# A second MLP's norm: an activation table loaded earlier, a residual summed one quarter at a time, and idle transposes in between

## The chip, the cores and the metric

The kernel runs on one core of one Trainium2 chip. The metric is the device time in microseconds (us) of one execution. The kernel before takes 2209.97 us, the median of three runs (2206.25 to 2210.57 us).

## What is computed

Two transformer layers one after the other, on 256 tokens of width 2048, in float32. The first is a hybrid mixer with an MLP; the second is this one, and the change sits at the seam between its attention and its MLP:

```python
def rmsnorm_2(x, g):
    xf = x.astype(jnp.float32)
    y = xf * lax.rsqrt(jnp.mean(xf * xf, axis=-1, keepdims=True) + EPS)
    return (y * g.astype(jnp.float32)).astype(x.dtype)

def sqrelu_mlp(x, w1, w2):
    return (jnp.square(jax.nn.relu(x @ w1)) @ w2).astype(x.dtype)

def second_block(x, ...):
    h = rmsnorm_2(x, norm_g[i, 0])
    h = fox_attention(h, fox_w_in[j], fox_b_f[j], fox_w_out[j])
    x = x + rmsnorm_2(h, norm_g[i, 1])
    h = sqrelu_mlp(rmsnorm_2(x, norm_g[i, 2]), mlp_w1[i], mlp_w2[i])
    x = x + rmsnorm_2(h, norm_g[i, 3])
```

So between the attention's last product (`fox_w_out`) and the MLP's first product (`mlp_w1`) there stand a norm of h over all 2048 columns, a sum, and the turning of x so that its columns lie on the partitions. The MLP's own norm (`norm_g[i, 2]`) is applied as a gain while x is turned; its root is put in later, on the MLP's output.

## The kernel before, in words

**Products.** A float32 product is made of three passes over parts in a reduced type: each weight is split into a high part (`wh`, ScalarE, `hi`, L634) and a low part (`wl`, VectorE, `lo`, L1155), and so are the activations (`XH` and `XL`, kept together as `XHL`). Weights come in chunks of 128x2048 (1 MB). There are four chunk slots, j = 0 to 3, and four chunks make one panel of 512 output columns. `raw` and `wl` share their memory, so a slot's next chunk is fetched by SyncE only when the product has used the slot (`chunk_used`). A panel's result stands in a pair of PSUM banks, `acc[o % 2]`.

**Order.** Every engine's order is written out by hand; the engines meet at semaphores, and each engine works strictly down its own list. `B_FOUT` are the four panels of `fox_w_out`; `B_M2` is the first panel of `mlp_w1`.

**The seam, engine by engine.** After the last `fox_w_out` matmul:
- ScalarE squares the last 512 columns straight from PSUM (`squares(2, 3)`, L677 and L678), takes the square root (`root`, L641), and then, for each quarter of x, copies the turned blocks with their gain into `XH` (`take_quarter`, L655). In between it makes the high parts of chunks 1, 2 and 3 (`hi`, L637). Chunk 0 is ready already.
- VectorE adds the squares up (L1173, L1174), multiplies the last panel of h by its gain (`fox_panel(3)`, L1928), takes the reciprocal (L1183), adds h to x in quarters of 512 columns (`fox_added`, L1937), and makes the low parts of the turned blocks (`low_quarter`, L1192) and of the chunks (L1158).
- TensorE turns x. A quarter is two pairs of blocks, eight transposes (`turn_quarter`, L2112). Then it runs the panel: sixteen k-tiles, each of twelve matmuls (L2066 to L2068), four k-tiles to a chunk.

In `first_panel` of before, for this MLP (m = 3, so `late` is false), quarters 0 and 1 are turned before the product, quarter 2 after chunk 0 and quarter 3 after chunk 1. Ahead of each chunk the product waits for both pairs of its quarter and for the chunk's low part:

```python
                for j in range(4):
                    wait_emptied(pe, ("xt", m, 2 * j))
                    wait_emptied(pe, ("xt", m, 2 * j + 1))
                    form(b, j, o % 2, j == 0, j == 3, 4 * j)
                    if not late and j < 2:
                        turn_quarter(m, j + 2)
```

ScalarE's order there is: take quarter 0, `hi` of chunk 1, take quarters 1 and 2, `hi` of chunk 2, take quarter 3, `hi` of chunk 3. VectorE's `lo` of chunk 2 stands behind its low parts of quarter 2, and `lo` of chunk 3 behind those of quarter 3. The change leaves these stretches as they are.

Of the kernel before, what the change touches and what calls it, by code (L numbers as in the profile page):

```python
# [18 lines left out]
P = 128  # L19
TOK = 256  # L20
NT = TOK // P
D = 2048
KT = D // P
# [41 lines left out]
ACT = mybir.ActivationFunctionType  # L65
# [5 lines left out]
def hybrid_then_fox(nc, x, g_mix, w_in, conv_w, conv_b, dt_bias, a_log, d_skip, g_ssd, g_q, g_k,  # L71
# [3 lines left out]
    with ctx:  # L75
        def sem(name):
            return ctx.enter_context(nc.semaphore(name))

        def sb(name, shape, dt=F32):
            return ctx.enter_context(nc.sbuf_tensor(name, shape, dt))  # L80


        ident = sb("ident", [P, P])
# [4 lines left out]
        rstd = sb("rstd", [P, 6, NT])  # L88
# [103 lines left out]
        acc = [[bank[0], bank[1]], [bank[2], bank[3]]]  # L192
# [5 lines left out]
        lo_ready = sem("lo_ready")  # L198
        chunk_used = sem("chunk_used")
# [213 lines left out]
        def wait_emptied(eng, name):  # L413

            b, n = uses[name]
            eng.wait_ge(side_free[b], n + 1)
# [129 lines left out]
        def landed(b, j):  # L546

            return 16 * b

        def split(b, j):  # L550

            return 4 * b + j - 3
# [72 lines left out]
        def _(act):  # L625
# [8 lines left out]
            def hi(b, j):  # L634

                act.wait_ge(raw_landed[j], landed(b, j))
                act.activation(slot(wh, b, j), slot(raw, b, j), ACT.Copy).then_inc(hi_ready, 1)  # L637
# [21 lines left out]
            def root(m, n):  # L659

                std(var_ready, n, std_ready, rstd[:, m, :], rstd[:, m, :])
# [18 lines left out]
            def squares(which, q):  # L680
                if which == 2:

                    act.wait_ge(chunk_used, 4 * (B_FOUT + q) + 4)
                    square_sums(which, q, [acc[(O_FOUT + q) % 2][t][:, :] for t in range(NT)])
                else:

                    act.wait_ge(sum_ready, 4 * (which - which // 3) + q + 1)
                    src = HB if which == 4 else X
                    square_sums(which, q, [src[:, t, 512 * q:512 * q + 512] for t in range(NT)])
# [434 lines left out]
                        squares(2, n - 1)  # L1124

            hi(B_M2, 0)
            squares(2, 3)
            root(4, 3)
            take_quarter(3, 0)
# [16 lines left out]
        def _(dve):  # L1146
# [51 lines left out]
            def low_quarter(m, q):  # L1198
                for n in (2 * q, 2 * q + 1):
                    low_pair(m, n)  # L1200
# [649 lines left out]
            for n in range(8):  # L1850
                for i in range(2):
                    k = 2 * n + i
# [57 lines left out]
            for n, (kind, col) in enumerate(FOX):  # L1910
# [7 lines left out]
                        take(*prev)  # L1918
                prev = (kind, fox_acc(n), seen.get(kind, 0), B_FOX + n)
                seen[kind] = seen.get(kind, 0) + 1  # L1920
            def fox_panel(q):

                cols, o = slice(512 * q, 512 * q + 512), O_FOUT + q
                dve.wait_ge(ssq_ready, 10 + q)
                if q == 0:
                    dve.wait_ge(g1_landed, 16)
                for t in range(NT):
                    dve.tensor_tensor(HB[:, t, cols], acc[o % 2][t][:, :], G1[:, cols], ALU.mult)\  # L1928
                       .then_inc(acc_freed[o % 2][t], 1)

            def fox_added(q):

                cols, o = slice(512 * q, 512 * q + 512), O_FOUT + q
                for t in range(NT):
                    dve.wait_ge(acc_freed[o % 2][t], o // 2 + 1)
                for t in range(NT):
                    ins = dve.scalar_tensor_tensor(out=X[:, t, cols], in0=HB[:, t, cols],  # L1937
                                                   scalar=rstd[:, 4, t:t + 1], in1=X[:, t, cols],
                                                   op0=ALU.mult, op1=ALU.add)
                ins.then_inc(sum_ready, 1)  # L1940
# [22 lines left out]
                        fox_panel(n - 1)  # L1963
            lo(B_M2, 0)
            mean_square(4, 13).then_inc(var_ready, 1)
            fox_panel(3)
            inverse_root(4, 3)

            fox_added(0)
            fox_added(1)  # L1970
            low_quarter(3, 0)
            lo(B_M2, 1)
            low_quarter(3, 1)
            fox_added(2)
# [6 lines left out]
            o = O_M2 + O_HALF + O_DOWN[1] + DOWN - 1  # L1981
# [28 lines left out]
        def _(pe):  # L2010
            def acc_wait(o, n=None):

                n = o // 2 if n is None else n
                if not (isinstance(n, int) and n == 0):
                    for t in range(2):
                        pe.wait_ge(acc_freed[o % 2][t], n)
# [43 lines left out]
            def k_tile(b, j, kk, o_par, first, last, k):  # L2060

                for f in range(4):
                    o = acc[o_par][f // 2][:, TOK * (f % 2):TOK * (f % 2 + 1)]
                    sh, sl = (slot(z, b, j)[:, kk, f * P:(f + 1) * P] for z in (wh, wl))
                    mh, ml = XH[:, k, :], XL[:, k, :]
                    pe.matmul(o, sh, mh, start=first and f % 2 == 0, stop=False, skip_group_check=True)  # L2066
                    pe.matmul(o, sh, ml, start=False, stop=False, skip_group_check=True)  # L2067
                    mm = pe.matmul(o, sl, mh, start=False, stop=last, skip_group_check=True)  # L2068
                return mm

            def warm(n):

                for i in range(n):
                    pe.transpose(acc[1][1][:, 0:P], ident[:, :], ident[:, :])

            def turn_first(n):

# [22 lines left out]
            def turn_quarter(m, q):  # L2100

                pe.wait_ge(sum_ready, 4 * (m - 1) + q + 1)
                for n in (2 * q, 2 * q + 1):
                    turn_pair(m, n)
# [9 lines left out]

            def first_panel(form, m, b, o, plan={}):

                late = m in (1, 2)
                if not late:
                    turn_quarter(m, 0)
                    turn_quarter(m, 1)  # L2120
                for j in range(4):
                    if j == 0:
                        acc_wait(o)

                    wait_emptied(pe, ("xt", m, 2 * j))
                    wait_emptied(pe, ("xt", m, 2 * j + 1))
                    form(b, j, o % 2, j == 0, j == 3, 4 * j)
                    if late and j == 1:
                        turn_quarter(m, 3)
                    if not late and j < 2:  # L2130
                        turn_quarter(m, j + 2)
                    side_work(plan, j)

            def panel(form, b, o, plan={}, slot=0):
                acc_wait(o)
# [51 lines left out]
            def mlp(m, b0, o0, u0):  # L2187
                for half in range(2):
                    b, o, u = b0 + half * B_HALF, o0 + half * O_HALF, u0 + half * U_HALF[0]
                    for n in range(UP):  # L2190
                        if half == 0 and n == 0:
                            first_panel(cols, m, b, o)
                        else:
                            for j in half_cols(b + n, o + up_acc(half, n)):
                                pass
                    if half:
                        for s in range(SLOTS):
                            pe.wait_ge(hl_ready, 2 * (u + s) + 2)
                            if s == UNITS[0]:
                                acc_wait(o + O_DOWN[1])  # L2200
                                acc_wait(o + O_DOWN[1] + 1)
                            if s in UNITS:
                                seven(m, b + UP, s, o + O_DOWN[1])
                            else:
                                eight(b + UP, s)
                    for n in range(2 * half, DOWN):
                        on = o + O_DOWN[half] + n
                        acc_wait(on)
                        for j in range(8):
                            if n == 0:  # L2210

                                pe.wait_ge(hl_ready, 2 * (u + up_acc(half, j + 1)) + 2)
                            if m == 3 and half == 1 and n == DOWN - 1 and j > 5:
                                continue
                            rows(b + UP + 2 * n + j // 4, j % 4, on % 2, j == 0, j == 7, 4 * j, hh, hl)
                            if half == 1 and m == 1 and j in ((3, 5) if n == 2 else (3,)):
                                turn_quarter(2, (n - 2) * 2 + j // 2 - 1)
                if m == 3:

                    rows(B_END - 1, 2, on % 2, False, False, 24, hh, hl, [0], None)  # L2220
                    rows(B_END - 1, 3, on % 2, False, True, 28, hh, hl, [0], first_tokens)
                    rows(B_END - 1, 2, on % 2, False, False, 24, hh, hl, [1])
                    rows(B_END - 1, 3, on % 2, False, True, 28, hh, hl, [1])
# [165 lines left out]
            def side_work(plan, n):  # L2389
                for name in plan.get(n, ()):  # L2390
                    fill(name)
# [66 lines left out]
```

## Time and profile before

| | |
|---|---|
| median of 3 runs | 2209.97 us (2206.25 to 2210.57) |
| profiled execution: span, first to last instruction | 2211.3 us |
| TensorE busy | 2187.9 us (99%) |
| VectorE busy | 1312.6 us (59%) |
| ScalarE busy | 989.2 us (45%) |
| DMA, mean over the span | 188 GB/s |
| seam: last `fox_w_out` matmul starts, first `mlp_w1` matmul starts | 1494.21 and 1503.27 us |

For the profiled execution only its span is shown, and no time of its own around it; the span is 1.3 us above the median of the runs. Times inside the execution are counted from the span's start. A row of a timeline gives the start, the length, the engine, the line of the kernel, and how many instructions of that kind are merged; brackets give the idle time before and what ended it.

### The profile page before, as it was taken

How to read it: one execution, taken by the hardware profiler on the slowest of the kernel's cores; microseconds unless marked ns; L12 is line 12 of the kernel's file. 1: busy time of each engine (PE TensorE's matmuls, PEld its weight loads, DVE VectorE, ACT ScalarE, POOL GpSimd, SP SyncE). 2: the span in 40 equal slices, each digit the busy share in tenths (PEclk: the TensorE clock that was granted, in tenths of full speed). 3: DMA queues.
4: the chain of work that ended last, by engine and by line, in shares of the span. 5: the costliest groups of instructions: out<-in, count | busy, mean ns of one | idle time of the engine just before them, and what ended most of it. 6: DMA issues, size and time to landing. Idle time of an engine off the chain costs nothing.

```text
span 2211.3 us, 27606 instructions
## 1 busy us (share of the span) xinstructions
PE 2187.9 (99%) x11798; PEld 1886.0 (85%) x11798; DVE 1312.6 (59%) x1541; ACT 989.2 (45%) x1117; POOL 28.5 (1%) x71
## 2 busy tenths in 40 slices
PE   9999999999999999999999999999999999999998
PEld 8988778988888888888898888888888888888887
DVE  5688665556544466676455655546555444666764
ACT  6453564444433344444434444534445333444442
POOL 1000000000000000000001110000000000000000
PEclk9999999999999999999999999999999999999999
DMA  7454435566555666665566655565765556665674
GB/s 245 153 169 161 156 133 186 176 190 191 192 197 197 194 192 190 190 192 195 186 192 200 186 188 169 177 196 160 221 198 191 190 192 196 195 190 185 204 248 151
DMA packets 280985, 415.46 MB, mean 188 GB/s; under 512 B 13284, under 2 KB 167056, under 8 KB 280608
## 3 DMA queue, kind: packets, MB, share of 16 engines
q1 hardware_dynamic: 279376, 409.89, 57.9%
q0 software_dynamic: 1456, 3.81, 0.6%
q8 instruction: 93, 1.52, 0.3%
q14 instruction: 28, 0.23, 0.0%
q10 hardware_dynamic: 32, 0.01, 0.0%
HBM read 409.47 MB, written 4.21 MB: 187 GB/s over the span
## 4 chain that ended last, share of the span: by engine, by line
PE 94%; DVE 3%; ACT 1%; issue 0%; DMA 0%; DVEq 0%; SPq 0%; ACTq 0%
PE bank L2053 24%; PE bank L2026 13%; PE bank L2028 13%; PE bank L2027 13%; PE bank L2055 12%; PE bank L2066 3%; PE bank L2068 2%; PE bank L2067 2%; PE bank L2145 2%; PE bank L2147 2%; PE bank L2146 2%; DVE wl L1158 1%; PE bank L2229 1%; PE bank L2112 1%; PE bank L2250 0%
## 5 line engine op out<-in xcount | busy, mean ns | idle before, releaser
L1158 DVE TENSOR_TENSOR wl<-raw,wh 128x2048 fp32r<-128x2048 f32 x376 | 860.2, 2290 | 483.3 <-ACT wh L637 482.2
L637 ACT ACTIVATE wh<-raw 128x2048 fp32r<-128x2048 f32 x376 | 720.7, 1918 | 514.5 <-DMA raw<-in_mlp_w_dram 160.9
L2053 PE MATMUL bank<-XHL,wh 128*128 128x512 f32 x2368 | 814.9, 392 | 0.0
L2055 PE MATMUL bank<-XHL,wl 128*128 128x256 f32 x2368 | 655.9, 277 | 0.0
L2053 PEld LDWEIGHTS bank<-XHL,wh 128*128 128x128 f32 x2368 | 444.7, 188 | 95.1 <-DVE wl L1158 1.4
L2055 PEld LDWEIGHTS bank<-XHL,wl 128*128 128x128 f32 x2368 | 444.6, 188 | 0.3
L2026 PE MATMUL bank<-wh,hh 128*128 128x512 f32 x768 | 299.0, 389 | 0.0
L2027 PE MATMUL bank<-wl,hh 128*128 128x512 f32 x768 | 298.8, 389 | 0.0
L2028 PE MATMUL bank<-wh,hl 128*128 128x512 f32 x768 | 298.8, 389 | 0.0
L2026 PE MATMUL bank<-wh,XHL 128*128 128x512 f32 x576 | 230.2, 400 | 1.3 <-DVE XHL L1166 1.3
L2028 PE MATMUL bank<-wh,XHL 128*128 128x512 f32 x576 | 225.1, 391 | 0.0
L2027 PE MATMUL bank<-wl,XHL 128*128 128x512 f32 x576 | 224.8, 390 | 0.0
L756 ACT ACTIVATE RB<-bank 128x256 f32<-128x256 f32 x120 | 39.6, 381 | 365.9 <-PE bank L2055 365.9
L1327 DVE TENSOR_TENSOR RB<-bank,RB 128x256 f32<-128x256 f32 x120 | 45.4, 419 | 215.3 <-ACT RB L756 215.1
L2028 PEld LDWEIGHTS bank<-wh,hl 128*128 128x128 f32 x768 | 144.2, 188 | 30.0
L2027 PEld LDWEIGHTS bank<-wl,hh 128*128 128x128 f32 x768 | 144.2, 188 | 29.8
L2026 PEld LDWEIGHTS bank<-wh,hh 128*128 128x128 f32 x768 | 144.2, 188 | 29.6
L2066 PE MATMUL bank<-XHL,wh 128*128 128x256 f32 x512 | 146.8, 287 | 3.9 <-DVE wl L1158 2.4
L2068 PE MATMUL bank<-XHL,wl 128*128 128x256 f32 x512 | 143.7, 281 | 0.0
L2067 PE MATMUL bank<-XHL,wh 128*128 128x256 f32 x512 | 143.6, 281 | 0.0
L2026 PEld LDWEIGHTS bank<-wh,XHL 128*128 128x128 f32 x576 | 108.6, 189 | 23.4 <-issue 2.0
L2028 PEld LDWEIGHTS bank<-wh,XHL 128*128 128x128 f32 x576 | 108.5, 188 | 23.4
(396 smaller groups left out, 1830.9 us busy)
## 6 DMA issues: line engine op xcount, KB each, us to landing
raw<-in_mlp_w_dram SPq DMA_DIRECT2D x128, 1024.0 KB, 5.3
raw<-in_w_up_dram SPq DMA_DIRECT2D x64, 1024.0 KB, 5.3
raw<-in_w_down_dram SPq DMA_DIRECT2D x64, 1024.0 KB, 5.0
raw<-in_fox_w_in_dram SPq DMA_DIRECT2D x48, 1024.0 KB, 5.1
raw<-in_w_in_dram SPq DMA_DIRECT2D x40, 1024.0 KB, 5.0
raw<-in_w_out_dram SPq DMA_DIRECT2D x16, 1024.0 KB, 5.0
raw<-in_fox_w_out_dram SPq DMA_DIRECT2D x16, 1024.0 KB, 5.0
raw<-in_w_in_dram SPq DMA_DIRECT2D x16, 256.0 KB, 7.0
```

What stands on the lines that cost most here:

```text
L637: act.activation(slot(wh, b, j), slot(raw, b, j), ACT.Copy).then_inc(hi_ready, 1)
L1158: dve.tensor_tensor(slot(wl, b, j), slot(raw, b, j), slot(wh, b, j).bitcast(F32), ALU.subtract)\
L1327: dve.tensor_tensor(RB[:, k, 0:TOK], acc[o % 2][k][:, 0:TOK], RB[:, k, TOK:], ALU.add)\
L2026: pe.matmul(o, sh, mh, start=first and kk == 0, stop=False)
L2027: pe.matmul(o, sh, ml, start=False, stop=False)
L2028: mm = pe.matmul(o, sl, mh, start=False, stop=last and kk == 3)
L2053: pe.matmul(bk[:, :].rearrange("p (s t) -> p s t", s=2), sh, XHL[:, k, :, :], start=k == 0, stop=False, skip_group_check=True)
L2055: mm = pe.matmul(bk[:, 0:TOK], sl, XH[:, k, :], start=False, stop=k == KT - 1, skip_group_check=True)
L2066: pe.matmul(o, sh, mh, start=first and f % 2 == 0, stop=False, skip_group_check=True)
L2067: pe.matmul(o, sh, ml, start=False, stop=False, skip_group_check=True)
L2068: mm = pe.matmul(o, sl, mh, start=False, stop=last, skip_group_check=True)
L2145: pe.matmul(bk[:, :], a[0], w[0], start=first, stop=False)
```

## The change

Five edits, all at this seam:
1. ScalarE runs a Sqrt on two columns of `rstd` that nothing needs yet (the result goes to slot 5), ahead of `squares(2, 3)`.
2. VectorE's `fox_panel(3)` is cut into its two token halves. It goes from ahead of the reciprocal to behind the sums: half 0 after `fox_added(0)`, half 1 after `fox_added(1)`.
3. VectorE's `low_quarter(3, 0)` moves from behind `fox_added(1)` to ahead of it.
4. TensorE runs 30 transposes of the identity into the panel's own PSUM bank, behind the last `fox_w_out` matmul.
5. This panel gets its own function, `normed_panel`. Only quarter 0 is turned ahead of the product; quarters 1, 2 and 3 are turned after k-tiles 1, 5 and 9. The product waits for one pair of blocks every two k-tiles.

```diff
             hi(B_M2, 0)
+            act.activation(rstd[:, 5, :], rstd[:, 2, :], ACT.Sqrt)
             squares(2, 3)
             root(4, 3)
...
-            def fox_panel(q):
+            def fox_panel(q, tokens=range(NT)):
...
-                for t in range(NT):
+                for t in tokens:
                     dve.tensor_tensor(HB[:, t, cols], acc[o % 2][t][:, :], G1[:, cols], ALU.mult)\
                        .then_inc(acc_freed[o % 2][t], 1)
...
             mean_square(4, 13).then_inc(var_ready, 1)
-            fox_panel(3)
             inverse_root(4, 3)
 
             fox_added(0)
+            fox_panel(3, [0])
+            low_quarter(3, 0)
             fox_added(1)
-            low_quarter(3, 0)
+            fox_panel(3, [1])
             lo(B_M2, 1)
...
+            def normed_panel(m, b, o):
+
+                acc_wait(o)
+                warm(30, acc[o % 2][1])
+                turn_quarter(m, 0)
+                for k in range(KT):
+                    if k % 2 == 0:
+                        wait_emptied(pe, ("xt", m, k // 2))
+                    if k % 4 == 0:
+                        pe.wait_ge(lo_ready, split(b, k // 4))
+                    mm = k_tile(b, k // 4, k % 4, o % 2, k == 0, k == KT - 1, k)
+                    if k % 4 == 3:
+                        mm.then_inc(chunk_used, 1)
+                    if k % 4 == 1 and k < 12:
+                        turn_quarter(m, k // 4 + 1)
```

`warm` gets the bank as an argument, and the MLP calls `normed_panel` in place of `first_panel` where m is 3.

VectorE, at the seam, from the sum of squares on. Before:

```order
L1173 TENSOR_REDUCE rstd<-ssq 128x2 [waits ssq_ready]
L1174 TENSOR_SCALAR rstd<-rstd 128x2 [waits dve_order]
L1928 TENSOR_TENSOR HB<-bank,G_116 128x512 [waits ssq_ready]
L1928 TENSOR_TENSOR HB<-bank,G_116 128x512
L1183 RECIPROCAL rstd<-rstd 128x2 [waits std_ready]
L1937 SCALAR_TENSOR_TENSOR X<-HB,rstd,X 128x512 [waits acc_freed11,acc_freed10,rs_ready]
L1937 SCALAR_TENSOR_TENSOR X<-HB,rstd,X 128x512
L1937 SCALAR_TENSOR_TENSOR X<-HB,rstd,X 128x512 [waits acc_freed01,acc_freed00]
L1937 SCALAR_TENSOR_TENSOR X<-HB,rstd,X 128x512
L1192 SCALAR_TENSOR_TENSOR XHL<-bank,gT,XHL 128x256 [waits gains_ready,xh_ready]
```

And of the change, from the same place:

```order
L1174 TENSOR_REDUCE rstd<-ssq 128x2 [waits ssq_ready]
L1175 TENSOR_SCALAR rstd<-rstd 128x2 [waits dve_order]
L1184 RECIPROCAL rstd<-rstd 128x2 [waits std_ready]
L1938 SCALAR_TENSOR_TENSOR X<-HB,rstd,X 128x512 [waits acc_freed11,acc_freed10,rs_ready]
L1938 SCALAR_TENSOR_TENSOR X<-HB,rstd,X 128x512
L1929 TENSOR_TENSOR HB<-bank,G_116 128x512 [waits ssq_ready]
L1193 SCALAR_TENSOR_TENSOR XHL<-bank,gT,XHL 128x256 [waits gains_ready,xh_ready]
L1193 SCALAR_TENSOR_TENSOR XHL<-bank,gT,XHL 128x256
L1193 SCALAR_TENSOR_TENSOR XHL<-bank,gT,XHL 128x256 [waits gains_ready,xh_ready]
L1193 SCALAR_TENSOR_TENSOR XHL<-bank,gT,XHL 128x256
L1938 SCALAR_TENSOR_TENSOR X<-HB,rstd,X 128x512 [waits acc_freed01,acc_freed00]
L1938 SCALAR_TENSOR_TENSOR X<-HB,rstd,X 128x512
```

The gain of the last panel has left the stretch between the variance and the reciprocal, and the low parts of the first quarter now stand ahead of the second sum. (Lines are one higher in the change.)

TensorE, around the turning of quarter 2. Before, it stands behind all four k-tiles of chunk 0, and all of chunk 1 follows before the product needs chunk 2:

```order
L2068 MATMUL bank<-XHL,wl 128x256
L2112 MATMUL bank<-ident,X 128x128 [waits side_free0,sum_ready]
L2112 MATMUL bank<-ident,X 128x128 x3
L2112 MATMUL bank<-ident,X 128x128 [waits side_free1]
L2112 MATMUL bank<-ident,X 128x128 x3
L2066 MATMUL bank<-XHL,wh 128x256 [waits lo_ready,side_free3,side_free2]
```

Of the change, the same quarter, and the first matmul of chunk 2, with k-tiles 6 and 7 between the two (24 matmuls, left out but for the first):

```order
L2114 MATMUL bank<-ident,X 128x128 [waits side_free0,sum_ready]
L2114 MATMUL bank<-ident,X 128x128 x3
L2114 MATMUL bank<-ident,X 128x128 [waits side_free1]
L2114 MATMUL bank<-ident,X 128x128 x3
L2068 MATMUL bank<-XHL,wh 128x256 [waits side_free3]
...
L2068 MATMUL bank<-XHL,wh 128x256 [waits lo_ready,side_free0]
```

Quarter 2 has moved from between chunks 0 and 1 into the middle of chunk 1. Quarter 3 has moved in the same way, into the middle of chunk 2. (Here L2068 to L2070 are the matmuls that before were L2066 to L2068.)

ScalarE's order changes only by the early Sqrt, which takes the table load with it. Before:

```order
L637 ACTIVATE wh<-raw 128x2048 [waits raw_landed0]
L677 ACTIVATE junk,ssq<-bank 128x512 [waits ssq_ready,chunk_used]
L678 ACTIVATE junk,ssq<-bank 128x512 [waits act_order]
L641 ACT_TABLE_LOAD
L641 ACTIVATE rstd<-rstd 128x2 [waits var_ready]
```

Of the change, there and on to the end of the panel:

```order
L637 ACTIVATE wh<-raw 128x2048 [waits raw_landed0]
L1127 ACT_TABLE_LOAD
L1127 ACTIVATE rstd<-rstd 128x2
L677 ACTIVATE junk,ssq<-bank 128x512 [waits ssq_ready,chunk_used]
L678 ACTIVATE junk,ssq<-bank 128x512 [waits act_order]
L641 ACTIVATE rstd<-rstd 128x2 [waits var_ready]
L655 ACTIVATE XHL<-bank,gT 128x256 [waits side_full0]
L655 ACTIVATE XHL<-bank,gT 128x256
...
L637 ACTIVATE wh<-raw 128x2048 [waits raw_landed2]
...
L637 ACTIVATE wh<-raw 128x2048 [waits raw_landed3]
```

The second load at L641 is gone, and none has come in at the squares. The high parts of chunks 2 and 3 still stand behind the takes of quarters 2 and 3.

## Rows read from the trace of the kernel before

**Rows 1.** The page: span, busy time, and the chain that ended last, by engine.
```profile
span 2211.3 us, 27606 instructions
PE 2187.9 (99%) x11798; PEld 1886.0 (85%) x11798; DVE 1312.6 (59%) x1541; ACT 989.2 (45%) x1117; POOL 28.5 (1%) x71
PE 94%; DVE 3%; ACT 1%; issue 0%; DMA 0%; DVEq 0%; SPq 0%; ACTq 0%
```

**Rows 2.** TensorE's waits: waiting line, releaser, us in total, times, longest.
```profile
PE bank L2112 <- DVE X L1937: 4.7, 1, 4.7
```

**Rows 3.** Timeline of the seam: start, us, engine, line, what, [idle before].
```profile
1494.21 0.39 PE L2028 MATMUL bank<-wh,XHL 128*128 128x512 f32 x1
...
1494.63 0.60 ACT L677 ACTIVATE junk<-bank 128x512 bf16<-128x512 f32 x1 [9.14 <-PE bank L2028]
...
1496.06 1.28 ACT L641 ACT_TABLE_LOAD   x1
...
1496.27 0.17 DVE L1174 TENSOR_SCALAR rstd<-rstd 128x2 f32<-128x2 f32 x1
1496.35 1.28 DVE L1928 TENSOR_TENSOR HB<-bank,G 128x512 f32<-128x512 f32 x2
1497.35 0.20 ACT L641 ACTIVATE rstd<-rstd 128x2 f32<-128x2 f32 x1
1497.59 0.17 DVE L1183 RECIPROCAL rstd<-rstd 128x2 f32<-128x2 f32 x1
1497.79 2.74 DVE L1937 SCALAR_TENSOR_TENSOR X<-HB,rstd,X 128x512 f32<-128x512 f32 x4
...
1499.26 3.67 PE L2112 MATMUL bank<-ident,X 128*128 128x128 f32 x16 [4.66 <-DVE X L1937]
1500.41 1.69 ACT L655 ACTIVATE XHL<-bank,gT 128x256 fp32r<-128x256 f32 x4 [2.85 <-PE bank L2112]
1501.28 1.73 DVE L1192 SCALAR_TENSOR_TENSOR XHL<-bank,gT,XHL 128x256 fp32r<-128x256 f32 x4 [0.76 <-ACT XHL L655]
...
1503.27 0.55 PE L2066 MATMUL bank<-XHL,wh 128*128 128x256 f32 x1 [0.34 <-DVE XHL L1192]
```

**Rows 4.** Windows of the seam: stretch, busy us (x instructions) by engine, PEclk, DMA.
```profile
1494.60:1499.20 4.60, 0.00 (x0) 0.00 (x0) 3.06 (x8) 2.86 (x6) 0.00 (x0) 0.86 0.73 225
1499.20:1503.20 4.00, 3.67 (x16) 3.27 (x16) 3.06 (x7) 2.78 (x5) 0.00 (x0) 0.50 0.01 4
1503.20:1504.70 1.50, 1.43 (x7) 1.46 (x8) 0.77 (x1) 1.50 (x4) 0.00 (x0) 0.50 0.00 0
```

**Rows 5.** Timeline of TensorE in the panel: first matmuls of stretches, quarters 2 and 3.
```profile
1504.69 0.31 PE L2066 MATMUL bank<-XHL,wh 128*128 128x256 f32 x1
...
1509.49 1.03 PE L2112 MATMUL bank<-ident,X 128*128 128x128 f32 x8
1510.28 0.36 PE L2066 MATMUL bank<-XHL,wh 128*128 128x256 f32 x1
...
1516.02 1.03 PE L2112 MATMUL bank<-ident,X 128*128 128x128 f32 x8
1516.81 0.36 PE L2066 MATMUL bank<-XHL,wh 128*128 128x256 f32 x1
...
1522.54 0.31 PE L2066 MATMUL bank<-XHL,wh 128*128 128x256 f32 x1
```

**Rows 6.** Timeline of ScalarE and VectorE behind the turning of quarters 2 and 3.
```profile
1510.12 1.57 ACT L655 ACTIVATE XHL<-bank,gT 128x256 fp32r<-128x256 f32 x4 [4.76 <-PE bank L2112]
1511.57 1.93 ACT L637 ACTIVATE wh<-raw 128x2048 fp32r<-128x2048 f32 x1
...
1513.53 2.29 DVE L1158 TENSOR_TENSOR wl<-raw,wh 128x2048 fp32r<-128x2048 f32 x1 [0.88 <-ACT wh L637]
...
1516.65 1.57 ACT L655 ACTIVATE XHL<-bank,gT 128x256 fp32r<-128x256 f32 x4 [3.15 <-PE bank L2112]
...
1518.10 3.73 ACT L637 ACTIVATE wh<-raw 128x2048 fp32r<-128x2048 f32 x2
...
1520.06 4.50 DVE L1158 TENSOR_TENSOR wl<-raw,wh 128x2048 fp32r<-128x2048 f32 x2 [0.87 <-ACT wh L637]
```

More of the change, by code:

```diff
@@ L2069, in k_tile, with warm @@
                 return mm
-            def warm(n):
+            def warm(n, bk=acc[1][1]):
                 for i in range(n):
-                    pe.transpose(acc[1][1][:, 0:P], ident[:, :], ident[:, :])
+                    pe.transpose(bk[:, 0:P], ident[:, :], ident[:, :])
             def turn_first(n):
@@ L2115, in first_panel @@
             def first_panel(form, m, b, o, plan={}):
[L2117 to L2120, printed above, removed]
                 for j in range(4):
@@ L2127, in first_panel @@
                     form(b, j, o % 2, j == 0, j == 3, 4 * j)
-                    if late and j == 1:
+                    if j == 1:
                         turn_quarter(m, 3)
-                    if not late and j < 2:
-                        turn_quarter(m, j + 2)
                     side_work(plan, j)
+            def normed_panel(m, b, o):
[12 more added lines that the diff above has]
+                        turn_quarter(m, k // 4 + 1)
             def panel(form, b, o, plan={}, slot=0):
@@ L2190, in mlp @@
                     for n in range(UP):
-                        if half == 0 and n == 0:
+                        if half == 0 and n == 0 and m == 3:
+                            normed_panel(m, b, o)
+                        elif half == 0 and n == 0:
                             first_panel(cols, m, b, o)
```

## The prediction

> **What bounds the kernel.** I read the page first. TensorE is busy 99% of the 2211.3 us, and 94% of the chain that ended last is TensorE's [rows 1]. So a microsecond counts only where TensorE itself waits. Its list of waits has one long entry: 4.7 us for the first sum of x, at the seam that the change is about [rows 2]. The timeline of that seam shows the chain that fills the hole [rows 3]: the squares from 1494.63, the table load at 1496.06, the root at 1497.35, the reciprocal at 1497.59, the first sum from 1497.79 (half of four instructions in 2.74 us), and the transposes from 1499.26. The windows show a second cost [rows 4]. The granted clock averages 0.86 in the hole and is 0.50 until 1504.7, which is the 1.2 GHz level: TensorE had stood still since 1494.6 when it fell. Third, I read the rest of the panel [rows 5, 6], because edit 5 moves transposes there and ScalarE and VectorE hang behind them.
>
> **The gain at the head of the panel.**
> - Table load and gain (edits 1 and 2). With the table in place the root follows the variance. That ends at 1496.27 + 0.17 = 1496.44; with the 0.04 us hand-over seen from root to reciprocal, the root takes 1496.48 to 1496.68 and the reciprocal starts near 1496.71, against 1497.59 [rows 3]. VectorE would still have been in `fox_panel(3)` until 1497.63, so both edits are needed for it. **0.88 us.** The early load itself lies in the 9.14 us in which ScalarE is idle anyway and costs nothing.
> - The 30 transposes (edit 4). Eight take 0.79 us at 2.4 GHz [rows 5], so 30 take 3.0 us, up to 3.3. They start at about 1494.4 and end by 1497.7. The first turn follows the start of the first sum by 1499.26 − 1497.79 = 1.47 us and so comes at 1498.4. They delay nothing and leave 0.7 us of idleness. If they hold the clock at 2.4 GHz, two things shrink. From the first transpose to the first take it is 1510.12 − 1509.49 = 0.63 us at that clock against 1500.41 − 1499.26 = 1.15 us [rows 3, 5, 6]: **0.52 us**. And the first seven matmuls, 1503.27 to 1504.69, take 1.42 us; at the pace of the 41 that follow, (1509.49 − 1504.69) / 41 = 0.117 us, they would take 0.82: **0.60 us**.
> - One pair of blocks awaited instead of two (edit 5): half of the 1.73 us of low parts [rows 3], **0.86 us**.
> - Quarter 1 was turned in the hole and is now turned between k-tiles 1 and 2: **−0.79 us** [rows 5]. Its sum (edit 3 puts it behind the first low parts) is there in time: the low parts end near 1501.6, two sums of 0.68 us end at 1503.0, and TensorE asks at 1503.8.
>
> Sum: 0.88 + 0.52 + 0.60 + 0.86 − 0.79 = **2.07 us**. The product starts near 1501.0, and k-tile 3 ends at 1507.4, where before it was 1509.49. Chunk 1's low part, now behind a sum and half a gain, is done at 1505.9 and the next low pair at 1506.8, 0.4 us before k-tile 4. That is the thinnest cover at the head.
>
> **What the same edit loses further on.** Behind the turning of a quarter hangs a chain that the edits do not shorten [rows 6]. For quarter 2 it runs: turned from 1509.49, taken from 1510.12, `hi` of chunk 2 from 1511.57, `lo` of chunk 2 from 1513.53 to 1515.82, or **6.33 us**. For quarter 3 it is 1516.02 to 1520.06 + 2.29 = 1522.35, again **6.33 us**. The product needs `lo` of chunk 2 at k-tile 8 and `lo` of chunk 3 at k-tile 12. Before, the transposes (0.79) and a whole chunk (1516.02 − 1510.28 = 5.74) covered each chain: 6.53 us, nearly nothing to spare. Now only the transposes and two k-tiles (half a chunk, 2.87) stand there: 3.66 us. So TensorE waits 6.33 − 3.66 = **2.7 us, twice**. In times:
> - Quarter 2 is turned at 1507.4 + 2.87 = 1510.3, which is 0.8 us later than before. `lo` of chunk 2 ends at 1516.6. TensorE has been ready since 1514.0.
> - K-tiles 8 and 9 end at 1519.5, and quarter 3 is turned 3.5 us later than before. `lo` of chunk 3 ends at 1525.85. TensorE has been ready since 1523.2. K-tile 12 starts at 1525.85, against 1522.54 [rows 5].
>
> That is **3.3 us later** than before: 2.07 gained, 2 x 2.67 lost. Nothing behind wins it back, since TensorE is the bound from there on. SyncE fetches a chunk when its slot is used: the next panel's chunks 0 and 1 start up to 2 us earlier, its chunks 2 and 3 as much later as that panel itself.
>
> The bounds of the terms: the two waits 2.4 to 3.0 us each; the gain 0.3 us either way, and without a held clock 1.1 less. The 3.0 comes from the 0.26 us by which the product started behind the end of the low parts in the hole [rows 3], which I have not added here; the 2.4 allows as much on the other side.
>
> **Forecast.** 2209.97 + 3.3 = **2213.3 us**, 0.15% slower, inside the 0.2% (4.4 us) that a measurement of this kernel can tell. The profiled span should be 2211.3 + 3.3 = 2214.6 us.
>
> **The rivals.**
> - *The clock falls in the new waits* (clearly slower; chance 0.17). Place: k-tiles 8 and 12, each behind 2.7 us without a matmul. For it: in the hole the clock fell with TensorE idle for about 3.3 us (0.86 over 4.6 us is 3.3 us at 1.00 and 1.3 at 0.50), and came back only at 1504.7, 5.4 us after work had resumed [rows 3, 4]. Against it: the waits are shorter, with dense work on both sides. Price of one fall: the seven slow matmuls cost 0.60 us as the low end; as the high end 5.4 us of work at 0.20 us a matmul (1.42 / 7), in which the fast pace needs 5.4 x 0.117 / 0.20 = 3.2, a loss of 2.2 us or a little more. Two falls: 3.3 + 4.4 = 7.7, so **2217.7 us**. It decides the sign of the verdict from 1.1 us of extra loss on. The Trainium skill, "TensorE: Matmul & The Clock Gate", section "HAM oscillation — how this bites in real kernels", says that waits between k-tiles put the clock back and that each following tile starts slow; by that rule both waits would pay, and this rival would be the forecast. No row of before shows waits of this size, so I keep it below.
> - *The identity transposes do not hold the clock* (chance 0.10). For it: 0.7 us of idleness ahead of the first turn and 1.7 us before the product. Against: the hole was wholly idle before. The price is the 0.52, and the product's matmuls slow from 1501.5 to 1504.7, 3.2 us at 0.20 instead of 0.117, 1.3 us: 3.3 + 1.8 = 5.1, **2215.1 us**.
> - *The late chains are hidden after all* (faster side; chance 0.08). `lo` of chunks 2 and 3 would have to be done when k-tiles 8 and 12 come up. Then only the head counts: −2.07, **2207.9 us**. Against it stands ScalarE's order, which keeps `hi` of chunk 2 behind the takes of quarter 2, and the 6.33 us of each chain.
> - *The early Sqrt saves nothing* (inside the forecast's case, chance 0.05): a load comes back at the root, because the squares want other tables. 0.88 is lost again: **2214.2 us**. The order shows no second load.
>
> **How the numbers follow.** The forecast has 0.60. Its own range is 2211.3 to 2215.3 (the bounds of the terms), with 1 to 2 us more on each side for the runs, which spread over 4.3 us. About a fifth of it lands beyond 2214.4. With the clock rival (nearly all slower) and half of the second, slower by over 0.2% gets 0.28. Faster by over 0.2%, below 2205.6, is left only to the tail of the third rival and the spread of the runs: 0.05. Within 0.2%: 0.67. The range of 8 in 10 reaches down into the third rival and up to the first: 2207.0 to 2218.0.
>
> **What would show it.** In the profile of the change: no table load at L641 and the reciprocal near 1496.7; a first turn near 1498.4 (times from the span's start, if the stretch ahead keeps its pace); PEclk at 1.00 up to the product; the first k-tile near 1501.0; quarter 1 turned without a wait. Then two waits of TensorE of about 2.7 us each, at the first matmuls of chunks 2 and 3, released by VectorE's low part of a weight chunk (L1159). The prediction is wrong if these waits are missing or under 1 us, or if PEclk falls in them.

## The result, and the profile after

The change is slower. Its median is 2215.18 us (2213.41 to 2218.57, six runs) against 2209.61 us before (2206.25 to 2211.64, six runs); the ratio is 1.0029 with a 95% interval of 1.0019 to 1.0038, which is 4 to 8 us (the two medians by themselves give 1.0025). The profiled execution has a span of 2213.4 us and a time of 2215.18 us, so 1.8 us lie around the span.

The page and TensorE's list of waits in the change (waiting line, releaser, us in total, times, longest):

```profile
span 2213.4 us, 27667 instructions
```

```profile
PE bank L2068 <- DVE wl L1159: 7.8, 4, 2.6
...
PE bank L2068 <- DVE XHL L1193: 1.4, 1, 1.4
...
PE bank L2114 <- DVE X L1938: 0.5, 1, 0.5
```

The long wait for the first sum, 4.7 us in [rows 2], has shrunk to 0.5 us behind the identity transposes. A new group stands at the top: TensorE waits for the low parts of weights. Of its 7.8 us, 2.4 in two waits are in the kernel before as well; the two new waits are 2.62 us each. Timeline of the seam in the change:

```profile
1493.21 3.44 PE L2076 MATMUL bank<-ident 128*128 128x128 f32 x30
1493.41 0.60 ACT L677 ACTIVATE junk<-bank 128x512 bf16<-128x512 f32 x1 [7.55 <-PE bank L2030]
...
1495.25 0.20 ACT L641 ACTIVATE rstd<-rstd 128x2 f32<-128x2 f32 x1 [0.43 <-DVE rstd L1175]
1495.49 0.17 DVE L1184 RECIPROCAL rstd<-rstd 128x2 f32<-128x2 f32 x1 [0.27 <-ACT rstd L641]
...
1497.16 1.09 PE L2114 MATMUL bank<-ident,X 128*128 128x128 f32 x8 [0.51 <-DVE X L1938]
1497.85 1.57 ACT L655 ACTIVATE XHL<-bank,gT 128x256 fp32r<-128x256 f32 x4 [2.40 <-PE bank L2114]
...
1499.66 0.38 PE L2068 MATMUL bank<-XHL,wh 128*128 128x256 f32 x1 [1.40 <-DVE XHL L1193]
1502.49 1.03 PE L2114 MATMUL bank<-ident,X 128*128 128x128 f32 x8
1509.02 1.03 PE L2114 MATMUL bank<-ident,X 128*128 128x128 f32 x8
1513.06 2.29 DVE L1159 TENSOR_TENSOR wl<-raw,wh 128x2048 fp32r<-128x2048 f32 x1 [0.87 <-ACT wh L637]
1515.50 0.55 PE L2068 MATMUL bank<-XHL,wh 128*128 128x256 f32 x1 [2.62 <-DVE wl L1159]
1519.67 1.04 PE L2114 MATMUL bank<-ident,X 128*128 128x128 f32 x8
1523.71 4.49 DVE L1159 TENSOR_TENSOR wl<-raw,wh 128x2048 fp32r<-128x2048 f32 x2 [0.88 <-ACT wh L637]
1526.15 0.36 PE L2068 MATMUL bank<-XHL,wh 128*128 128x256 f32 x1 [2.62 <-DVE wl L1159]
```

These rows answer to [rows 3, 5, 6]. The stretch ahead of the seam was 1.22 us shorter in this execution (the first square stands at 1493.41 instead of 1494.63), so I count from that square in what follows:

| us after the first square | before | change | moved |
|---|---|---|---|
| reciprocal | 2.96 | 2.08 | −0.88 |
| first take | 5.78 | 4.44 | −1.34 |
| first matmul of the product | 8.64 | 6.25 | −2.39 |
| quarter 2 turned | 14.86 | 15.61 | +0.75 |
| quarter 3 turned | 21.39 | 26.26 | +4.87 |
| first matmul of chunk 3 ("seam") | 27.91 | 32.74 | +4.83 |
| first matmul of the next panel ("panel") | 33.41 | 38.27 | +4.86 |

The head is 2.39 us faster. Then come two waits of 2.62 us, at chunks 2 and 3. The granted clock (windows: stretch, busy us by engine, PEclk, DMA share, GB/s) shows the rest; where it drops from 1.00 to 0.50, that is called a fall in what follows:

```profile
1494.60:1498.00 3.40, 2.89 (x27) 2.65 (x25) 2.51 (x6) 0.57 (x4) 0.00 (x0) 1.00 0.95 293
...
1512.00:1514.00 2.00, 0.88 (x8) 0.68 (x6) 1.13 (x2) 1.03 (x1) 0.00 (x0) 1.00 0.01 4
1514.00:1517.00 3.00, 1.50 (x7) 1.53 (x8) 1.35 (x1) 0.00 (x0) 0.00 (x0) 0.66 0.91 290
1517.00:1520.00 3.00, 3.00 (x23) 3.00 (x23) 0.00 (x0) 0.00 (x0) 0.00 (x0) 0.77 0.16 57
...
1523.00:1526.00 3.00, 0.53 (x5) 0.33 (x3) 2.29 (x2) 2.47 (x2) 0.00 (x0) 1.00 0.36 99
```

With the identity transposes in the hole the granted clock stays at 1.00, 2.4 GHz, where [rows 4] had 0.86 and then 0.50. But it falls to 1.2 GHz near the end of the first new wait and stays there over k-tile 8. Behind the second wait it does not fall. From chunk 2's first matmul to the turning of quarter 3 it takes 4.17 us (1519.67 − 1515.50).

### The profile page after: what moved, and what is told of

Its sections match the earlier page's. It is cut to its first block, busy times and chain, and to the rows that moved or that the text cites. A ratio compares the mean times of both kernels' runs of the same rounds, so it can differ in the third digit from the quotient of the medians.

```text
span 2213.4 us, 27667 instructions
## 1 busy us (share of the span) xinstructions
PE 2187.7 (99%) x11828; PEld 1885.9 (85%) x11828; DVE 1312.8 (59%) x1541; ACT 989.6 (45%) x1118; POOL 28.9 (1%) x71
## 4 chain that ended last, share of the span: by engine, by line
PE 94%; DVE 4%; ACT 2%; issue 0%; POOL 0%; DVEq 0%; POOLq 0%; ACTq 0%
PE bank L2055 24%; PE bank L2028 13%; PE bank L2030 13%; PE bank L2029 13%; PE bank L2057 12%; PE bank L2068 3%; PE bank L2157 2%; PE bank L2070 2%; PE bank L2069 2%; PE bank L2158 2%; PE bank L2159 2%; DVE wl L1159 1%; PE bank L2243 1%; PE bank L2114 1%; ACT wh L637 1%; PE bank L2264 0%
## 5 line engine op out<-in xcount | busy, mean ns | idle before, releaser
L2068 PE MATMUL bank<-XHL,wh 128*128 128x256 f32 x512 | 147.1, 287 | 10.5 <-DVE wl L1159 7.8
L2070 PE MATMUL bank<-XHL,wl 128*128 128x256 f32 x512 | 143.7, 281 | 0.0
```

## The experiments

All are read by the same two stretches, seam and panel. Both are counted from the first square, whose time from the span's start is in the second column: the seam ends with the first matmul of chunk 3, the panel with the first matmul of the next panel. The granted clock and the waits are from each kernel's own profile. The ratios are to the runs of before that were made beside each kernel, whose medians are 2208.6, 2209.0 and 2209.6 us.

| kernel | first square at | product starts | seam | panel | median, us | ratio to before (95%) |
|---|---|---|---|---|---|---|
| before | 1494.63 | 8.64 | 27.91 | 33.41 | 2208.6 to 2209.6 | 1 |
| change | 1493.41 | 6.25 | 32.74 | 38.27 | 2215.18 | 1.0029 (1.0019 to 1.0038) |
| chunks first | 1490.05 | 6.25 | 25.86 | 31.30 | 2206.57 | 0.9990 (0.9981 to 0.9999) |
| head only | 1489.59 | 7.23 | 26.27 | 31.75 | 2206.67 | 0.9991 (0.9982 to 1.0000) |
| no transposes | 1493.19 | 6.87 | 35.00 | 40.54 | 2217.48 | 1.0037 (1.0023 to 1.0050) |
| filled waits | 1492.76 | 6.24 | 31.57 | 37.30 | 2212.93 | 1.0017 (1.0008 to 1.0026) |
| both | 1492.76 | 6.24 | 24.75 | 30.41 | 2205.81 | 0.9986 (0.9977 to 0.9995) |
| chunk 2 only | 1492.66 | 6.24 | 28.73 | 35.89 | 2211.28 | 1.0011 (1.0002 to 1.0020) |
| no early Sqrt | 1491.18 | 7.12 | 33.68 | 39.41 | 2215.71 | 1.0035 (1.0021 to 1.0049) |
| change, again | 1492.77 | 6.25 | 31.50 | 38.64 | 2216.01 (one run) | |

### Chunks first

The weight parts of chunks 2 and 3 go ahead of the takes and the low parts of quarters 2 and 3. With them the sum of quarter 3, `fox_added(3)`, comes to stand behind chunk 2's low part and quarter 2's low parts, and the loops of the MLP leave out chunk 3, which is made already (not shown). Nothing else differs from the change.

```diff
             take_quarter(3, 1)
-            take_quarter(3, 2)
             hi(B_M2, 2)
+            take_quarter(3, 2)
+            hi(B_M2, 3)
             take_quarter(3, 3)
...
             fox_added(2)
-            fox_added(3)
-            low_quarter(3, 2)
             lo(B_M2, 2)
+            low_quarter(3, 2)
+            fox_added(3)
+            lo(B_M2, 3)
             low_quarter(3, 3)
```

> The change, with the high and low parts of chunks 2 and 3 put ahead of the takes and low parts of quarters 2 and 3 (on ScalarE and VectorE). My measure is the seam: from the first square of the last fox_w_out panel (L677) to the first matmul of chunk 3; it is 27.91 us before and 32.74 us in the change. Theory A (the two waits come from the weight parts that stand behind the turning of quarters 2 and 3, and the clock fell because of the first wait): both waits of 2.62 us go, the clock stays at 1.00, the seam is 25.8 us, and the run is 2 us below before and 6 to 7 us below the change. Rival B (the product loses time because transposes now stand inside it, or because chunks are fetched at other times): the seam stays above 30 us and the run above before.

The seam is 25.86 us, the waits at chunks 2 and 3 are gone, and the clock does not fall in the panel (the window is the whole product):

```profile
1496.30 0.39 PE L2070 MATMUL bank<-XHL,wh 128*128 128x256 f32 x1 [1.40 <-DVE XHL L1194]
...
1503.95 2.29 DVE L1160 TENSOR_TENSOR wl<-raw,wh 128x2048 fp32r<-128x2048 f32 x1
...
1505.76 1.03 PE L2116 MATMUL bank<-ident,X 128*128 128x128 f32 x8
...
1510.17 2.29 DVE L1160 TENSOR_TENSOR wl<-raw,wh 128x2048 fp32r<-128x2048 f32 x1
...
1512.30 1.04 PE L2116 MATMUL bank<-ident,X 128*128 128x128 f32 x8
```

```profile
1496.30:1521.40 25.10, 25.10 (x217) 25.10 (x218) 19.08 (x25) 11.70 (x16) 0.00 (x0) 1.00 0.41 127
```

Chunk 2's low part (from 1503.95) is now begun before quarter 2 is turned (1505.76), and chunk 3's (from 1510.17) before quarter 3 (1512.30); they end 0.5 and 0.2 us behind these, over 3 us before the product needs them. Transposes still stand inside the product and its chunks are still fetched when a slot is used, so rival B falls. With its waits gone, the change is faster than before by the 2.1 us that its head was reckoned at (2.05 on the seam and by the medians, 2.11 on the panel). It is 8.6 us below the change by the medians, where 6 to 7 was expected and the panels differ by 6.97; the 1.6 us between are not explained.

### Head only

The kernel before, with the early Sqrt, the 30 transposes and the gain moved, but before's panel.

```diff
             hi(B_M2, 0)
+            act.activation(rstd[:, 5, :], rstd[:, 2, :], ACT.Sqrt)
             squares(2, 3)
...
             mean_square(4, 13).then_inc(var_ready, 1)
-            fox_panel(3)
             inverse_root(4, 3)
...
             low_quarter(3, 0)
+            fox_panel(3)
             lo(B_M2, 1)
...
                 if not late:
+                    acc_wait(o)
+                    warm(30, acc[o % 2][1])
                     turn_quarter(m, 0)
```

> The kernel before with the early Sqrt, the 30 identity transposes and the last panel's gain moved behind the low parts of quarter 0, but with before's panel: quarters 0 and 1 turned ahead, 2 and 3 between whole chunks. Theory A: the head gains 0.88 (root) + 0.5 (clock during the turning) + 0.6 (clock in the first matmuls) = 2.0 us, and since the chunks' order is before's, no wait appears at chunks 2 and 3: seam 25.9 us against 27.91, run 2 us below before. Rival C (the head's gain is not real or is given back by the weight parts, which lie on the path already): the seam stays within 0.5 us of 27.9.

The seam is 26.27 us, 1.64 below before, so the head's gain is real without edit 5. It is 0.4 us less than expected: I had left out that the gain, now behind the low parts of quarter 0, puts off VectorE's work for quarter 2.

```profile
1496.82 0.36 PE L2067 MATMUL bank<-XHL,wh 128*128 128x256 f32 x1 [1.06 <-DVE XHL L1193]
1502.91 1.09 PE L2113 MATMUL bank<-ident,X 128*128 128x128 f32 x8 [0.20 <-DVE X L1938]
```

TensorE waits 0.20 us for that quarter's sum. The rest of the difference lies in chunk 0 as well, which takes 6.09 us here with the wait, where I had reckoned with 5.6. Its second and third k-tiles take 1.42 and 1.41 us, where the fast k-tiles of chunk 0 before take 1.36, at a granted clock of 1.00 in both; what sets this pace no run shows.

### No transposes

```diff
                 acc_wait(o)
-                warm(30, acc[o % 2][1])
                 turn_quarter(m, 0)
```

> The change without its 30 identity transposes. Theory A: TensorE is idle for nearly 4 us in the hole, the clock falls there to 0.50 and stays low into the first k-tiles, so that the product starts 6.8 us after the first square instead of 6.25, and the seam is 1.1 to 1.8 us longer than the change has without a fall in its waits (31.4), that is 32.5 to 33.2 us. Rival D (the transposes do nothing for the clock): PEclk reads the same as in the change through the hole and the seam is within 0.3 us of the change's.

Rival D falls: the clock is low from the end of the hole into the product. Windows of this kernel:

```profile
1493.20:1496.60 3.40, 0.00 (x0) 0.00 (x0) 1.64 (x5) 1.57 (x5) 0.00 (x0) 1.00 0.68 173
1496.80:1503.40 6.60, 5.28 (x23) 4.91 (x24) 4.95 (x10) 3.48 (x5) 0.00 (x0) 0.50 0.16 60
1503.60:1509.00 5.40, 5.40 (x50) 5.40 (x49) 4.32 (x8) 1.57 (x4) 0.00 (x0) 1.00 0.00 0
```

My size was too small. The product starts at 6.87 as expected, but the seam is 35.00 us, above the 32.5 to 33.2 expected, which had no fall in the waits. Both this execution and the change's have one, in the first wait, so 35.00 − 32.74 = 2.26 us compares like with like. Of that, 2.09 us are there when chunk 2 starts (24.18 us after the square against 22.09; 1.98 against the change's repeat), before the fall costs anything; the other 0.17 is k-tiles 8 and 9, slower here (4.34 us against 4.17). So the transposes are worth about 2 us, above the 1.1 to 1.8 expected. The product now starts 1.8 us sooner than in the kernel before, and more of it lies in the slow stretch: its first two k-tiles take 1504.54 − 1500.06 = 4.48 us instead of 2.83.

```profile
1500.06 0.58 PE L2068 MATMUL bank<-XHL,wh 128*128 128x256 f32 x1 [0.99 <-DVE XHL L1193]
1504.54 1.04 PE L2114 MATMUL bank<-ident,X 128*128 128x128 f32 x8
```

### Filled waits

```diff
                 for k in range(KT):
+                    if k in (8, 12):
+                        acc_wait(o + 1)
+                        warm(20, acc[(o + 1) % 2][1])
                     if k % 2 == 0:
```

> The change with 20 more identity transposes ahead of k-tile 8 and 20 ahead of k-tile 12, into a bank that is free then; 20 take 2.2 us, less than the 2.62 us waits. Theory A: the waits for the low parts stay where they are (chunk 2 starts 22 us after the first square), but the clock does not fall, so the 1.3 us that the twelve slow matmuls of the change cost are saved: seam 31.4 us against 32.74, run about 3.5 us above before. Rival E (slow matmuls behind the wait come from something else than an idle TensorE, the fetch of chunks for instance): PEclk falls there again, and the seam stays at 32.7 us.

The seam is 31.57 us, 1.17 below the change's, and no fall of the clock lies in this panel:

```profile
1512.17 2.35 PE L2076 MATMUL bank<-ident 128*128 128x128 f32 x20
1514.94 0.36 PE L2068 MATMUL bank<-XHL,wh 128*128 128x256 f32 x1 [0.43 <-DVE wl L1159]
1517.85 1.03 PE L2114 MATMUL bank<-ident,X 128*128 128x128 f32 x8
1521.55 2.35 PE L2076 MATMUL bank<-ident 128*128 128x128 f32 x20
1524.33 0.36 PE L2068 MATMUL bank<-XHL,wh 128*128 128x256 f32 x1 [0.43 <-DVE wl L1159]
```

```profile
1499.00:1530.00 31.00, 30.14 (x256) 29.72 (x257) 19.17 (x25) 11.69 (x16) 0.00 (x0) 1.00 0.33 103
```

The chunks start when they did (22.18 us after the square; the low part sets it), but chunk 2's first two k-tiles now take 2.91 us instead of 4.17. Rival E falls: it was the idle TensorE. This kernel is the prediction's forecast made real. It has both waits, filled, and no fall, and it is 3.66 us longer than before on the seam, 3.89 on the panel, and its ratio is 1.0017.

### Chunk 2 only

```diff
-            take_quarter(3, 2)
             hi(B_M2, 2)
+            take_quarter(3, 2)
...
-            fox_added(3)
-            low_quarter(3, 2)
             lo(B_M2, 2)
+            low_quarter(3, 2)
+            fox_added(3)
             low_quarter(3, 3)
```

> The change with only chunk 2's high and low part put ahead of quarter 2's take and low parts; chunk 3's stay behind quarter 3's. Theory A: the two waits are independent. The one at chunk 2 goes, the one at chunk 3 stays at 2.6 us; quarter 3 is turned 22.25 us after the first square, 6.33 us later the low part of chunk 3 is done: seam 28.7 us, or 1.3 us more where the clock falls in that wait. Rival G (one common cause, ScalarE or the fetch of chunks being late over the whole panel): the wait at chunk 3 shrinks or grows with the first one, and the seam is below 27 or still above 31 us.

The seam is 28.73 us. The wait at chunk 2 is gone and the one at chunk 3 has its full size, so the two are independent and rival G falls. The seam is as expected, but the clock did something that I had not thought of:

```profile
1521.39 0.36 PE L2068 MATMUL bank<-XHL,wh 128*128 128x256 f32 x1 [2.71 <-DVE wl L1159]
```

```profile
1518.70:1521.30 2.60, 0.00 (x0) 0.00 (x0) 2.35 (x2) 2.01 (x2) 0.00 (x0) 1.00 0.52 123
1521.40:1522.00 0.60, 0.60 (x5) 0.60 (x6) 0.60 (x1) 0.00 (x0) 0.00 (x0) 1.00 1.01 352
1522.20:1525.40 3.20, 3.20 (x18) 3.20 (x17) 1.24 (x1) 0.00 (x0) 0.00 (x0) 0.50 0.37 130
```

It was at 1.00 through the whole wait and for 0.7 us of dense work behind it, and fell then. The seam misses that; the panel has it, at 35.89 us: chunk 3 takes 7.16 us instead of 5.53.

### No early Sqrt

```diff
             hi(B_M2, 0)
-            act.activation(rstd[:, 5, :], rstd[:, 2, :], ACT.Sqrt)
             squares(2, 3)
```

> The change without the early Sqrt, so that the table is loaded at the root again. Theory A: the reciprocal starts 2.96 us after the first square instead of 2.08, everything behind it moves by 0.88 us, and the waits at chunks 2 and 3 stay at 2.62: seam 33.6 us with one fall of the clock in the waits as in the change, 32.3 without. Rival H (the waits absorb what the head loses, since the weight parts would be ready anyway): the seam stays at 32.7 us or below, with shorter waits.

```profile
1492.61 1.28 ACT L641 ACT_TABLE_LOAD   x1
1493.90 0.20 ACT L641 ACTIVATE rstd<-rstd 128x2 f32<-128x2 f32 x1
1494.13 0.17 DVE L1183 RECIPROCAL rstd<-rstd 128x2 f32<-128x2 f32 x1 [1.15 <-ACT rstd L641]
```

The first square is at 1491.18, so the reciprocal starts 2.95 us after it. The product starts at 7.12 (0.87 later) and the seam is 33.68 (0.94 more than the change's, with the same single fall). The load is worth what the first term said. Rival H falls: the waits absorb nothing, because the chains hang behind the product's own progress.

### The change, again

> The change itself, profiled once more, to see what belongs to the kernel and what to the execution. Theory A: both waits of 2.62 us at the same places, the head as before to 0.05 us; whether the clock falls in a wait, and in which, may differ, each fall being worth about 1.3 us: seam 31.4, 32.7 or 34.0 us. Rival I (the fall always follows the first wait): 32.7 us again.

Same head, same two waits, other fall:

```profile
1514.97 0.36 PE L2068 MATMUL bank<-XHL,wh 128*128 128x256 f32 x1 [2.71 <-DVE wl L1159]
...
1524.27 0.55 PE L2068 MATMUL bank<-XHL,wh 128*128 128x256 f32 x1 [2.62 <-DVE wl L1159]
```

```profile
1515.00:1517.70 2.70, 2.70 (x24) 2.70 (x25) 0.00 (x0) 0.00 (x0) 0.00 (x0) 1.00 0.77 263
...
1524.10:1527.30 3.20, 3.03 (x14) 3.06 (x15) 2.23 (x2) 0.00 (x0) 0.00 (x0) 0.50 0.72 247
```

Here the clock falls in the second wait and not in the first. It falls at about 1524.0, at the end of that wait, so its cost lies behind the end of the seam, which is why the seam reads 31.50; the panel is 38.64. Rival I falls. Over the profiles with 2.6 to 2.7 us waits that stay empty (the change twice, no transposes, no early Sqrt, chunk 2 only), each shows exactly one fall at them: in the first wait three times, in the second once, and just behind the single wait of chunk 2 only.

### Both

Chunks first, and quarter 1 back in the hole. ScalarE's order is that of "chunks first".

```diff
             fox_added(0)
-            fox_panel(3, [0])
-            low_quarter(3, 0)
             fox_added(1)
-            fox_panel(3, [1])
+            low_quarter(3, 0)
             lo(B_M2, 1)
             low_quarter(3, 1)
             fox_added(2)
-            fox_added(3)
-            low_quarter(3, 2)
             lo(B_M2, 2)
+            fox_panel(3)
+            low_quarter(3, 2)
+            fox_added(3)
+            lo(B_M2, 3)
             low_quarter(3, 3)
...
                 turn_quarter(m, 0)
+                turn_quarter(m, 1)
...
-                    if k % 4 == 1 and k < 12:
+                    if k % 4 == 1 and 1 < k < 12:
                         turn_quarter(m, k // 4 + 1)
```

> The head's gains and the chunks' order together: the change with the high and low parts of chunks 2 and 3 ahead of the takes and low parts of quarters 2 and 3, and with quarter 1 summed and turned in the hole again (the last panel's gain goes behind the low part of chunk 2). Theory A: the product starts 6.25 us after the first square as in the change, there is no transposing of quarter 1 in the product (0.8 us), no wait at chunks 2 and 3, PEclk 1.00: seam 24.9 to 25.1 us, against 25.86 with only the chunks' order mended, 26.27 with the head alone and 27.91 before; run 3 us below before. Rival F (the hole is then bound by ScalarE's takes, so that turning quarter 1 early delays quarter 0's blocks): the product starts later than 6.5 us and the seam is not below 25.8.

```profile
1496.50 1.09 PE L2115 MATMUL bank<-ident,X 128*128 128x128 f32 x8 [0.51 <-DVE X L1939]
1497.83 1.09 PE L2115 MATMUL bank<-ident,X 128*128 128x128 f32 x8 [0.23 <-DVE X L1939]
...
1499.00 0.39 PE L2069 MATMUL bank<-XHL,wh 128*128 128x256 f32 x1
```

The product starts 6.24 us after the square (1492.76), as without quarter 1 in the hole; the second eight transposes fit in front of it. Rival F falls. The seam, 24.75 us, is a little below the 24.9 to 25.1 expected. The panel is 30.41 us, 3.00 below before, and the run is 0.9986 of before (0.9977 to 0.9995). It has the lowest median of all versions and the clearest gain over before; chunks first and head only have medians below before too, with intervals that end at 0.9999 and 1.0000.

## Why the prediction was right, and where not

- **The head.** Forecast 0.88 + 0.52 + 0.60 + 0.86 − 0.79 = 2.07 us. The root's term is 0.88 in the change's profile and 0.87 by the run without the early Sqrt. Product start: forecast 2.26 earlier, measured 2.39. Together the terms came out as quarter 2 turned 0.75 us later, forecast 0.8. The transposes' term was reckoned against the kernel before (0.52 + 0.60); inside the changed order they are worth about 2 us. Edits 2 and 3, and the wait for one pair instead of two, were not taken out one by one, so their shares are argued from the rows.
- **The two waits.** Forecast 2.7 us each from a chain of 6.33 us and a cover of 3.66. Measured 2.62 us of idleness each, and the chains are 6.33 us again (1509.02 to 1513.06 + 2.29, and 1519.67 to 1523.71 + 2.29). That they come from the order of the weight parts is shown by "chunks first" and "chunk 2 only", which take away both and the first alone. As lateness a wait is somewhat dearer than its idle time: chunk 2 starts 6.48 us after quarter 2 is turned (0.15 behind the end of the chain), and 3.70 in "chunks first", so 2.78 us. That is the hand-over that the prediction named at its upper bound and did not add; with it the filled kernel's seam grows by 3.66 where 3.3 was forecast.
- **The clock in the waits** is the step that failed, and by its own last sentence ("or if PEclk falls in them") the prediction is wrong there. The forecast took the waits as shorter than the hole, with dense work on both sides, and left the clock at 2.4 GHz, so the forecast has no term for a fall; the fall got 0.17. It fell once in every one of the five profiles that had an empty wait of this size, and in none of "chunks first", "head only" and "both", which have no such wait, nor of "filled waits". The price was inside its bounds (0.60 to 2.2 us): k-tiles 8 and 9 with the turn behind them take 4.17 us slow and 2.82 fast (the change's repeat), so 1.35 us, and a fall behind chunk 3's start costs 7.16 − 5.53 = 1.63. It is neither of my cases alone: one fall, where the rival had two. Forecast 3.3 plus one fall gives 4.7 to 4.9 us. The panel moved by 4.86, and by 5.23 in the repeat, so the closeness of the first figure is partly luck. The Trainium skill, "TensorE: Matmul & The Clock Gate", section "HAM oscillation — how this bites in real kernels", tells of a kernel in which waits of about 3 to 5 us between k-tiles put the clock back at every k-tile. I had applied that to waits of 2.7 us, which is more than the section states. As a direction it was the better guide: here waits of 2.62 to 2.71 us did put the clock back, though at one of the two and not at each.
- **The number.** 2213.3 us was forecast and 2215.18 measured, within 2207.0 to 2218.0. Against before's later median, 2209.61, the kernel moved by 5.6 us where 3.3 was forecast; one fall is 1.35 to 1.63 of these 2.3 us. Without falls it would probably have stayed within 0.2%, as the filled kernel does (1.0017, up to 1.0026). With them the result lies beyond the 0.2% bound by the ratio (1.0029) and the medians (1.0025), though the interval begins at 1.0019: the case that had 0.28.
- **Two sums of the prediction do not come out.** The terms' lower bound is 2 x 2.4 − 2.37 = 2.4 us, so 2212.4 and not 2211.3, which comes out only if the 1.1 us of a clock that is not held are taken off; they can only add to the time. And a fifth of 0.60, 0.17 and half of 0.10 add up to about 0.34 for slower by over 0.2%, not 0.28. Neither touches the forecast.
- **The profiled spans.** 2211.3 and 2213.4 us differ by 2.1 us only, though the panel alone cost 4.86. The seam began 1.22 us earlier, and another 1.5 us were won behind it, where the kernels are the same. What won it is not known. The spans of single executions do not weigh a change of this size; the medians and the panel do.

What stays open: the medians differ by 5.6 us and the panel by 4.9; the interval holds both. How often an execution has one fall and how often none or two is not counted. The change's slowest run, 2218.57 us, has a granted clock of 0.995 over its whole span, where the profiled one with three falls (near 37 us, near 310 us, and in the first wait) has 0.996, so it probably had more; "one of the two" is what five profiles show and no rule. Why the k-tiles of one execution take 1.36 us and those of another 1.41 at the same granted clock is open as well.

## What to carry to other kernels

When transposes or takes are interleaved into a product in finer steps, look up what else stands behind them on the other engines: moving a step later by half a chunk moves everything that its engine does after it, and the cover must be as long as that whole chain (here 6.33 us against 3.66). Put the weight parts, whose inputs have landed (the DMA share is 0.01 from 1499.2 us on, [rows 4]), ahead of the work that waits for TensorE. Reckon a new wait of some 2.6 us on TensorE as up to 4.4 us here (2.78 late, and up to 1.63 for a fall), unless it is filled.

## What the hardware showed that was not expected

A wait is priced twice, and the second part differs between executions of the same kernel. In the change and its repeat the same two waits, equal to 0.1 us, cost the clock once at the first and once at the second. In "chunk 2 only" the clock fell 0.7 us after dense work had resumed. Shorter waits seem to do it too. In every kernel TensorE waits about 2 us at 36 us and 1.3 us at 310 us; near these places the clock is low in some executions and not in others, and between 9 us and the last 6 us of the span none of the ten profiles has a fall anywhere but near these two places, in the hole, or at the new waits (windows of the kernel before, then of "chunks first"):

```profile
37.10:40.30 3.20, 3.20 (x17) 3.20 (x16) 3.20 (x3) 0.87 (x1) 0.00 (x0) 0.50 0.94 311
...
310.20:313.30 3.10, 3.10 (x8) 2.42 (x9) 2.18 (x2) 2.16 (x3) 0.00 (x0) 0.50 0.00 0
```

```profile
37.10:40.30 3.20, 3.20 (x31) 3.20 (x30) 3.20 (x3) 0.56 (x1) 0.00 (x0) 1.00 0.91 316
...
310.20:313.30 3.10, 3.10 (x15) 2.58 (x14) 2.70 (x3) 0.15 (x1) 0.00 (x0) 1.00 0.00 0
```

The same code starts 17 matmuls in a stretch of 3.2 us with the clock low and 31 with it high. That is probably part of why runs of one kernel spread over 4 us, but no fill was tried at these two places, so that these waits cause the falls is not shown.
